# Query weights of a PEER layer through two pairs of buffers, first expert rows in other tiles

## The reference

```python
def reference(x, c, ctx, c_ctx, w_mod, ..., w_query, sub_keys, expert_u, expert_v, g_final):
    # one layer here: x and ctx are (1, 256, 2048) float32
    mod = jax.nn.silu(c) @ w_mod[l] + b_mod[l]
    sh1, sc1, ga1, sh2, sc2, ga2 = jnp.split(mod[:, None, :], N_MOD, axis=-1)
    ...                                              # context scan states, latent mixing
    y = jnp.concatenate([fourier_mix(four, g_fourier[l]), y_m], axis=-1) @ w_out[l]
    x = x + ga1 * y
    h2 = modulate(rmsnorm(x, g_norm_ffn[l]), sh2, sc2)
    x = x + ga2 * peer(h2, w_query[l], sub_keys[l], expert_u[l], expert_v[l])
    return rmsnorm(x, g_final)

def peer(...):                                       # xb: 128 tokens
    q = (xb @ w_query).reshape(PEER_BLOCK, PEER_HEADS, 2, PEER_QDIM // 2)
    s = jnp.einsum('thpd,hpnd->thpn', q, sub_keys)
    sv, si = lax.top_k(s, PEER_TOPK)
    ...                                              # 16 x 16 candidates per head
    top_s, pos = lax.top_k(cand, PEER_TOPK)
    idx = jnp.take_along_axis(cidx, pos, axis=-1)    # 16 experts per head and token
    gate = jax.nn.softmax(top_s.astype(jnp.float32), axis=-1)
    act = jax.nn.gelu(jnp.einsum('thkd,td->thk', expert_u[idx], xb).astype(jnp.float32))
    return jnp.einsum('thk,thkd->td', (gate * act).astype(xb.dtype), expert_v[idx])
```

## Time and profile before

| | before |
|---|---|
| median of 3 runs | 2023.39 us (2022.85 to 2025.05) |
| the profiled execution, its own time | 2022.52 us |
| its span | 2020.7 us |
| PE busy | 1647.9 us (82%) |
| DVE busy | 1112.4 us (55%) |
| ACT busy | 381.8 us (19%) |
| POOL busy | 695.9 us (34%) |
| moved by DMA | 723.61 MB, mean 358 GB/s |

### The profile page before, as it was taken

One profiled execution on the slowest core, in us unless ns is written; L12 is line 12 of the kernel. 1 busy time (PEld: TensorE's weight loads), 2 busy tenths in 40 slices (PEclk: granted clock), 3 DMA queues, 4 the chain that ended last, 5 costly groups with the idle time before them and its releaser, 6 DMA issues.

```text
span 2020.7 us, 13865 instructions
## 1 busy us (share of the span) xinstructions
PE 1647.9 (82%) x4619; PEld 774.8 (38%) x4619; DVE 1112.4 (55%) x1862; ACT 381.8 (19%) x1124; POOL 695.9 (34%) x572
## 2 busy tenths in 40 slices
PE   3899999998999587799997777777777777777776
PEld 0446444556446476343332222222222222222332
DVE  1158863666545858334354664655647646556444
ACT  2011003114102000222222212212213122122112
POOL 1000100000100423666663535535445455354541
PEclk7899999999999798899999999999999999999999
DMA  9979764543983977999999999999999999999996
GB/s 381 407 287 342 275 224 167 196 179 124 380 307 125 371 306 321 373 422 423 423 422 422 423 421 422 422 422 422 422 422 422 422 423 422 423 422 422 423 422 267
DMA packets 136777, 723.61 MB, mean 358 GB/s; under 512 B 10218, under 2 KB 10554, under 8 KB 69635
## 3 DMA queue, kind: packets, MB, share of 16 engines
q0 software_dynamic: 92784, 614.83, 74.2%
q1 hardware_dynamic: 43760, 107.82, 14.2%
q10 hardware_dynamic: 162, 0.08, 0.0%
HBM read 720.56 MB, written 2.13 MB: 358 GB/s over the span
## 4 chain that ended last, share of the span: by engine, by line
DMA 43%; PE 31%; DVE 12%; POOL 9%; issue 3%; SPq 1%; ACT 1%; DVEq 0%; POOLq 0%
DMA ring<-in_expert_u,acc 17%; PE ps L867 11%; DMA ring<-in_expert_v,acc 10%; DMA qh<-in_expert_u,acc 7%; POOL ring L413 6%; PE ps L992 4%; PE ps L1132 3%; DVE ring L1528 3%; DMA ring<-in_w_query 3%; DMA ring<-in_w_mod 2%; DMA H<-in_expert_v,acc 2%; PE ps L774 1%; PE ps L863 1%; PE ps L861 1%; POOL VX L413 1%
## 5 line engine op out<-in xcount | busy, mean ns | idle before, releaser
L1132 PE MATMUL ps<-ring,wg 128*128 128x512 f32 x1184 | 545.1, 606 | 163.8 <-DMA ring<-in_expert_v,acc 163.8
L1528 DVE SCALAR_TENSOR_TENSOR ring<-ring,A 128x2048 f32<-128x2048 f32 x177 | 404.1, 2293 | 381.7 <-DMA ring<-in_expert_u,acc 381.4
L1132 PEld LDWEIGHTS ps<-ring,wg 128*128 128x128 f32 x1184 | 216.9, 192 | 490.6 <-issue 307.3
L413 POOL DMA_INDIRECT ring<-in_expert_u,acc x177 | 243.7, 1377 | 393.2 <-DVE ring L1528 323.4
L1132 PE MATMUL ps<-H,wg 128*128 128x512 f32 x576 | 262.5, 600 | 67.0 <-DMA H<-in_expert_v,acc 67.0
L867 PE MATMUL ps<-ring,H 128*128 128x512 f32 x512 | 225.0, 598 | 2.2 <-ACT VX L517 2.2
L692 ACT ACTIVATE wg<-K,VX 128x128 f32<-128x128 f32 x256 | 102.8, 402 | 654.0 <-PE ps L1132 652.3
L413 POOL DMA_INDIRECT ring<-in_expert_v,acc x148 | 175.4, 1185 | 106.1 <-PE ps L1132 62.2
L1132 PEld LDWEIGHTS ps<-H,wg 128*128 128x128 f32 x576 | 104.6, 190 | 223.4 <-issue 141.8
L1155 DVE SCALAR_TENSOR_TENSOR acc<-ring,vec,acc 128x512 f32<-128x512 f32 x240 | 180.4, 752 | 11.7 <-DMA ring<-in_w_mod 3.3
L360 POOL DMA_DIRECT2D ring<-in_w_mod x32 | 28.7, 896 | 443.1 <-DVE acc L1155 342.0
(11 more groups left out here) (227 smaller groups left out, 1272.7 us busy)
## 6 DMA issues: line engine op xcount, KB each, us to landing
ring<-in_w_mod POOLq DMA_DIRECT2D x32, 2048.0 KB, 9.3
ring<-in_w_mod SPq DMA_DIRECT2D x16, 2048.0 KB, 21.7
ring<-in_w_in SPq DMA_DIRECT2D x15, 2048.0 KB, 12.4
ring<-in_w_out SPq DMA_DIRECT2D x8, 2048.0 KB, 14.1
ring<-in_w_query SPq DMA_DIRECT2D x8, 2048.0 KB, 20.2
ring<-in_expert_u,acc POOLq DMA_INDIRECT x177, 24.5
ring<-in_expert_v,acc POOLq DMA_INDIRECT x148, 25.1
B<-in_ctx SPq DMA_DIRECT2D x2, 1024.0 KB, 20.3
```

The source lines that it names most:

```text
L413: nc.gpsimd.indirect_dma_start(rows_, None, table, bass.IndirectOffsetOnAxis(ap=eidx[:, rank:rank + 1], axis=0)).then_inc(loaded, 16)
L1132: ins = mm(ps[:, 4 * b + n, :], diag[:, r % 4, :], v_rows[r % V_SLOTS][:, n * CH:(n + 1) * CH], start=k == 0, stop=k == BLOCK_RANKS - 1, s ...
L1528: v.scalar_tensor_tensor(out=rows_u, in0=rows_u, scalar=1.0, in1=A[:, r // BLOCK_RANKS, :], op0=ALU.mult, op1=ALU.mult, accum_out=dots[:, ...
```

## The change

`w_query`'s chunks alternate between two pairs of buffers: chunks 0 and 2 go to `W[2]` and `W[3]` with semaphores of their own (`q_ld`), chunks 1 and 3 to `W[0]` and `W[1]`. Chunk 0 is issued when VectorE is done with the last two halves of the modulation (`m_free` 31 and 32), chunk 1 when TensorE is done with the halves of `w_out`'s last chunk (`w_free` 39 and 40), chunk 2 at `w_free` 41 and 42, which TensorE gives when it is done with the halves of chunk 0, and chunk 3 at 43 and 44, the halves of chunk 1. Before, chunk n waited for the halves of the chunk just ahead of it, `w_free` 39 and 40 for chunk 0 to 45 and 46 for chunk 3.

Since `W[2]` and `W[3]` are rows 4 to 7 of `ring`, the first 36 U ranks use four other slots: `VX`, `gy`, the first 2048 columns of `KT`, and `gwork`, a new tile that also holds the gate tiles `gsb`, `t1`, `t2` and `negm` (in use only in the first half). From rank 36 on, U has seven slots: `ring` 4 to 7, `qh`, `VX`, `gwork`. `ga2` and the final norm's weights go into `KT` and `gy` only after that, in POOL's queue behind the gathers of U rank 43 and V rank 15 (`load_last_rows`).

```diff
--- before.py
+++ after.py
@@ -50,10 +50,11 @@
 SPREAD_ORDER = (0, 1, 2, 3)
 RANKS = TB * PH * TOPK
 BLOCK_RANKS = PH * TOPK
-EARLY = 5
+EARLY_SLOTS = (4, 7, 8, 6)
+LATE_SLOTS = (0, 1, 2, 3, 5, 4, 6)
 LEAD = 36
 LAG = 4
-U_SLOTS, V_SLOTS = 6, 7
+U_SLOTS, V_SLOTS = 9, 7
 CLOSING = 24
 SOFT_FIRST = 4
 SOFT_AT = {40: 4} | {g * TOPK + 3: g + 1 for g in range(4, TB * PH - 1)}
@@ -104,7 +105,7 @@
 
 def u_slot(r):
 
-    return r % EARLY if r < LEAD else (r - LEAD) % U_SLOTS
+    return EARLY_SLOTS[r % len(EARLY_SLOTS)] if r < LEAD else LATE_SLOTS[(r - LEAD) % len(LATE_SLOTS)]
 
 
 def lag_behind(u):
@@ -167,15 +168,14 @@
         vec = sb("vec", [P, V_ALL])
         shT = sb("shT", [P, 2, KB])
         gT = sb("gT", [P, 2, KB])
-        gsb = sb("gsb", [NG, 2 * T])
-        t1 = sb("t1", [40, 2 * T])
-        t2 = sb("t2", [40, 2 * T])
-        negm = sb("negm", [40, T])
+        gwork = sb("gwork", [P, D])
         bg = sb("bg", [NG, 1])
         uT = sb("uT", [P, 6, 40])
         st = sb("st", [P, 64])
         small = sb("small", [P, 16])
 
+        gsb, t1, t2 = gwork[0:NG, 0:2 * T], gwork[0:40, 2 * T:4 * T], gwork[0:40, 4 * T:6 * T]
+        negm = gwork[0:40, 6 * T:7 * T]
         ident = K[:, C_ID:C_ID + P]
         ones32 = K[:, C_ONE:C_ONE + 32]
         eps = K[:, C_EPS:C_EPS + 1]
@@ -225,7 +225,7 @@
         sums = VXf[:, D + 1280:D + 1296]
         eidx = flat(acc)[:, 0:256].bitcast(U32)
         u_rows = [*(ring[:, 4 + i, :] for i in range(4)), VXf[:, 0:D],
-                  qh[:].rearrange("p a b t -> p (a b t)")]
+                  qh[:].rearrange("p a b t -> p (a b t)"), gwork[:], gy[:], KTf[:, 0:D]]
         v_rows = [*(ring[:, i, :] for i in range(4)), Hf[:, 0:D], Hf[:, D:2 * D], modrow[:]]
         wgf = flat(wg)
         diag = wgf[:, 0:4 * P].rearrange("p (s n) -> p s n", s=4)
@@ -245,6 +245,7 @@
         S = {n: sem(n) for n in names}
         w_ld = [sem(f"w_ld{i}") for i in range(2)]
         m_ld = [sem(f"m_ld{i}") for i in range(2)]
+        q_ld = [sem(f"q_ld{i}") for i in range(2)]
         a_ld = [sem(f"a_ld{i}") for i in range(4)]
         u_ld = [sem(f"u_ld{i}") for i in range(U_SLOTS)]
         v_ld = [sem(f"v_ld{i}") for i in range(V_SLOTS)]
@@ -324,10 +325,19 @@
                 for i, kh in enumerate(HALVES):
                     sp.wait_ge(S["w_free"], 32 + 2 * n + i - 1)
                     load(kh, w_out[0], kh, slice(n * CH, (n + 1) * CH))
-            for n in range(4):
+            def load_query(n, kh):
+                base, loaded = (2, q_ld) if n % 2 == 0 else (0, w_ld)
+                sp.dma_start(W[base + kh], w_query[0][kh * KH * P:(kh + 1) * KH * P,
+                                                      n * CH:(n + 1) * CH].rearrange(
+                    "(k p) n -> p k n", p=P)).then_inc(loaded[kh], 16)
+
+            for kh in range(2):
+                sp.wait_ge(S["m_free"], 2 * (MODB - 1) + kh + 1)
+                load_query(0, kh)
+            for n in range(1, 4):
                 for i, kh in enumerate(HALVES):
-                    sp.wait_ge(S["w_free"], 40 + 2 * n + i - 1)
-                    load(kh, w_query[0], kh, slice(n * CH, (n + 1) * CH))
+                    sp.wait_ge(S["w_free"], 36 + 2 * n + i + 1)
+                    load_query(n, kh)
             for b in range(TB):
                 for n in range(4):
                     sp.wait_ge(S["final_ready"], 4 * b + n + 1)
@@ -374,10 +384,13 @@
             pool.dma_start(gy[:, FW:D], g_mlstm.to_broadcast([P, FW])).then_inc(S["ld_gy"], 16)
             load_from(MODB_SCAN + 1, MODB_LATE)
 
-            def spread(r, dst, loaded):
-
+            def store_row(r):
                 pool.dma_start(mod_dram[r:r + 1, :], modrow[32 * r:32 * r + 1, :]
                                ).then_inc(S["st_mod"], 16)
+
+            def spread(r, dst, loaded):
+
+                store_row(r)
                 pool.wait_ge(S["st_mod"], 16 * (SPREAD_ORDER.index(r) + 1))
                 pool.dma_start(dst, mod_dram[r:r + 1, :].to_broadcast([P, D])
                                ).then_inc(S[loaded], 16)
@@ -403,11 +416,15 @@
 
             pool.wait_ge(S["g2_ready"], 1)
             pool.wait_ge(S["modb_free"], MODB)
-            spread(3, ga2, "ld_ga2")
+            store_row(3)
             pool.wait_ge(S["keys_psum"], 16)
-            pool.dma_start(gy[:], g_final.rearrange("(a d) -> a d", a=1).to_broadcast([P, D])
-                           ).then_inc(S["ld_gfin"], 16)
-
+
+            def load_last_rows():
+                pool.wait_ge(S["u_free"], LEAD)
+                pool.wait_ge(S["st_mod"], 16 * 4)
+                pool.dma_start(ga2, mod_dram[3:4, :].to_broadcast([P, D])).then_inc(S["ld_ga2"], 16)
+                pool.dma_start(gy[:], g_final.rearrange("(a d) -> a d", a=1).to_broadcast([P, D])
+                               ).then_inc(S["ld_gfin"], 16)
 
             def gather(table, rows_, rank, loaded):
                 nc.gpsimd.indirect_dma_start(
@@ -436,6 +453,8 @@
                 gather_u(LEAD + i)
                 gather_v(2 * i)
                 gather_v(2 * i + 1)
+                if i == len(LATE_SLOTS):
+                    load_last_rows()
             r = 2 * (LEAD - LAG)
             for u in range(r + LAG, RANKS):
                 gather_u(u)
@@ -1046,12 +1065,11 @@
                     kh = HALVES[part]
                     kk = kh * KH + k
                     if k == 0:
-                        n = 0
-                        pe.wait_ge(w_ld[kh], 16 * (12 + n + kh))
+                        pe.wait_ge(q_ld[kh], 16)
                         if part == 0 and b == 1:
                             pe.wait_ge(S["qtok_ready"], h + 1)
                     ins = mm(ps[:, h, 0:T], h2T[:, kk, b * P:(b + 1) * P],
-                             W[kh][:, k, h * T:(h + 1) * T], start=step == 0, stop=step == KB - 1)
+                             W[2 + kh][:, k, h * T:(h + 1) * T], start=step == 0, stop=step == KB - 1)
                     if step == KB - 1:
                         ins.then_inc(S["qtok_psum"], 1)
                 return ins
@@ -1100,13 +1118,17 @@
                 if n == 3:
                     pe.wait_ge(S["q_free"], 2)
                 for part, kh in enumerate(HALVES):
-                    pe.wait_ge(w_ld[kh], 16 * (12 + n + kh))
+                    if n == 2:
+                        pe.wait_ge(q_ld[kh], 32)
+                    else:
+                        pe.wait_ge(w_ld[kh], 16 * (12 + n // 2 + kh))
+                    wq = W[(2 if n == 2 else 0) + kh]
                     for j in range(4):
                         for k in range(KH):
                             kk = kh * KH + k
 
                             ins = mm(ps[:, 2 * (n % 2) + j // 2, (j % 2) * T:(j % 2 + 1) * T],
-                                     W[kh][:, k, j * P:(j + 1) * P], h2T[:, kk, :],
+                                     wq[:, k, j * P:(j + 1) * P], h2T[:, kk, :],
                                      start=part == 0 and k == 0 and j % 2 == 0,
                                      stop=part == 1 and k == KH - 1, skip_group_check=True)
                     ins.then_inc(S["w_free"], 1)
```

## The result

| | before | after |
|---|---|---|
| median of 4 runs each | 2023.22 us (2022.85 to 2025.05) | 1996.28 us (1993.86 to 1997.31) |
| ratio of after to before, 95% interval | | 0.9864 (0.9852 to 0.9876) |
| the profiled execution, its own time | 2022.52 us | 1993.86 us |
| its span | 2020.7 us | 1992.1 us |
| PE busy | 1647.9 us | 1639.7 us |

The change takes 1.4% off, 27 us between the medians. The forecast was 1991.0 us, with a range from 1981 to 2003. The spans of the two profiled executions differ by 28.6 us.

The account below looks back on a forecast made before the run. The prediction took the DMA's stream of gathers at 422 to 423 GB/s as the bound, so its start counts: 36.5 us earlier less 5.0 for broadcasts is 31.5, 2022.5 to 1991.0 us; range 1981 to 2003 us.

Parts of the forecast that it names:

- Chunk 0 early: Start of the query projection: the 1.97 us wait goes and matmuls run faster; gain 2.0 to 3.7 us, taken as 3.0.
- Chunk 1 early, no wait for scores: Query projection: chunk 1 lands before TensorE needs it; TensorE's 18.98 us and VectorE's 15.34 us waits go.
- Dots 0 to 15: VectorE's first dots: four ranks at its own pace of 2.26 us, twelve at the shared 3.23; 47.8 us, until 714.7.
- Dots 16 to 31: VectorE's dots after pick 2: between 36.1 us (VectorE alone) and 47.8 (shared pace); taken as 44, until 770.1.
- Chunks 2 and 3: Last query chunks: chunk 3 done at 762.4, its scores at 765.6, before dots end at 770.1, so dots set the start.
- Rival 3: Chunk 3's weights come late, scores at 785, rank 36 lands at 791: 2001 us; chance 0.13.
- The late stream: Gathers from rank 36 on: POOL no longer waits for dot 35; rank 36 lands at 780.8, 36.5 us before 817.3.
- It goes on: Late stream at the eighth V: its data can run 2 to 3 us before the queue empties; nothing charged.
- rival 2: The stream begins early but runs dry at the eighth V, DMA empty for 5 to 12 us: 1999 us; chance 0.12.
- The slower rival: TensorE stays at the lower clock for V rows after idling; 20 such rows would give 2057 us; chance 0.04.
- The broadcasts: Two 1.05 MB row loads, formerly in idle time, now stand in the full stream and cost 5.0 us.
- The seventh late slot: The extra U slot in the late stream is worth nothing where the DMA is already full.

Follow-up runs that it names:

- e5: The change, but chunk 0's halves issued late, as before, with the other chunks at their new times: 1998.45 us, ratio to before 0.9876.
- e3: The changed kernel with each half of w_query loaded at its old time, slots and buffers as changed: 2030.68 us, ratio to before 1.0035.
- e7: The changed kernel with ring rows as slots from U rank 20 on, six slots in place of four: 1985.97 us, ratio to before 0.9808.
- e2: The changed kernel without the two broadcast loads and the waits for them: 1988.74 us, ratio to before 0.9828.
- e6: The changed kernel with six late U slots instead of seven, gwork left out: 1994.54 us, ratio to before 0.9845.
- e1: The changed kernel run again unaltered: 1993.29 us, ratio to before 0.9847.

## Why the prediction was right, and where its steps were off

The measured 1996.28 lies in the range, 5.3 us above the forecast, and the likeliest case is the one that happened. By its steps, in the profile after, counted from the first query matmul (628.71, before 632.40) so that the 3.7 us ahead of it are out:

- **Chunk 0 early: 3.0 us forecast, 3.9 measured.** Pick 0 starts 10.9 us after the first query matmul (639.59), before 14.8 (647.20). It is a little above the upper bound of 3.7. How much of it reaches the end is open: e5 puts it at 3.9 by medians and at 1 to 2 by its profile.
- **Chunk 1 early, no wait for scores: as forecast.** The waits of 18.98 and 15.34 us are gone. e3 shows that all of the gain hangs on the early loads of the four chunks together (37.4 us), and e5 that some 4 us of that or less are chunk 0's.
- **Dots 0 to 15: 47.8 us forecast, 51.6 measured.** This is the step that failed most. I took the shared pace for all ranks behind the first four. But gather 4 can be issued only behind dot 0, at 664.85, and it shares the DMA with the gathers ahead of it and with chunk 2's weights (issued at 654.0 and 661.0, landed at 671.5 and 694.5). It lands in 10.5 us while dots 1 to 3 need 6.6: a wait of 4.11 at rank 4, where with five slots ranks 4 and 5 had waited 0.55 and 1.07. Rank 20's gather, issued behind dot 16 in the same way but with an almost idle DMA, took 7.3 us. The landings of these two, and the DMA at the time:

```profile
DMA to landing us min/median/max: 10.5/10.5/10.5
665.00:675.00 10.00, 10.00 (x48) 8.81 (x47) 6.22 (x6) 0.00 (x0) 7.35 (x4) 1.00 1.03 404
...
DMA to landing us min/median/max: 7.3/7.3/7.3
726.00:730.00 4.00, 4.00 (x20) 3.54 (x19) 4.00 (x5) 0.10 (x1) 2.17 (x1) 1.00 0.09 34
```

- **Dots 16 to 31: 44 us forecast, 45.8 measured,** within the bounds. The lower bound of 36.1 was nearly the right price for enough slots: e7 has 35.4, a dot every 2.21 us.
- **Chunks 2 and 3: done by 765.6 forecast, 756 measured.** Rival 3, weights late next, did not come: no wait ahead of either chunk. The weights were in fact much earlier than in the sum: chunk 2's halves landed at 671.5 and 694.5 (687 and 711 forecast) and chunk 3's at 717.8 and 728.1 (734 for the first). It did no harm, since the dots set the start.
- **The late stream: 36.5 us forecast, 30.1 measured.** Rank 36 was issued 2.4 us behind dot 31's end (771.06), not 1.3, for POOL was itself busy: four gathers ahead took 2.11 to 2.99 us each beside dots. Its rows, the yardstick, landed 10.0 us later, at 783.5: 33.8 us before 817.3, or 30.1 without the 3.7 ahead of the first query matmul. (Rank 38's dot, the first in the late stream that waited for its rows, gives 31.1: 798.42 against 833.26 before.) The 6.4 that are missing are the dots (3.8 and 1.8), POOL (1.1) and rank 36's landing (0.6: 10.0 us for 9.4 in the sum), less the 0.9 of chunk 0.
- **It goes on: right.** POOL stood 8.61 us at the eighth V and the DMA stayed at 421 GB/s; rival 2 had its wait but not its price. The slower rival did not come either. TensorE had idled 36.59 us and its clock was 0.51 in the window up to 797, the lower level (1.2 GHz), but 1.00 in the one from 797, and the DMA stayed full.
- **The broadcasts: 5.0 us forecast, 4.6 measured** (e2).
- **The seventh late slot: nothing, as forecast** (e6).

Together: 30.1 less 5.0 is 25.1, which is what the two profiles show when counted from the first query matmul (24.9). So part of the nearness to the forecast is luck: in the profiled pair, the 3.7 us ahead of the changed code make up for more than half of the 6.4 that the steps fell short. The medians give the change 26.9 us in the first measurement and 29.6 in the second (e1), against 31.5 forecast.

Two rules were weighed. The first is the fit of 2.0 us plus bytes over 436 GB/s for a transfer (the Trainium skill, "DMA: Bandwidth & Descriptors", section "Anatomy of one DMA — SWDGE (gpsimd) path", an estimate of 4.4 us for a gather). The prediction set it against landings of 8.2 and 10.2 us, but both were of gathers that shared the DMA. The fairest case after is the very first gather, issued at 651.79 into an idle DMA: it landed in 5.8 us, the shortest in that profile and still 1.4 above the estimate. Where it mattered the fit does not hold: gather 4 took 10.5 us and gather 35 took 8.5.

The second is the lock-out of GpSimd (the Trainium skill, "SBUF — State Buffer", section "SBUF: two separate sides"). It goes with what the issues show, 0.94 us alone and 1.9 to 3.0 beside dots. But for a VectorE operation with two SBUF inputs, as the dots are, that section names a conflict only with a GpSimd operation that reads SBUF, and whether the issue of a gather does so no run here shows; nor does any isolate the port as the cause.

## What to carry to other kernels

Where a stream at the limit of the DMA ends the kernel, ask only when it becomes full, and count bytes and idle time up to there: beside gathers of 8 KB rows at 324 GB/s the loads of 2 KB rows got some 90 here, so they belong ahead of the gathers. Count the slots of a ring against the order of the engine that frees them: one slot less cost 27.5 us here, most of it because the last gather fell behind a long step. Buffers that a change takes away may be free again a few steps later; giving them back brought another 9 us (e7).

## What the runs showed of the hardware that was not expected

- How long an indirect gather of 1.05 MB takes from issue to landing hangs on what else is under way: 5.8 us into an idle DMA with no dots running (rank 0 after), 7.3 us into an almost idle one beside dots (rank 20 after, 34 GB/s), 10.5 us beside other gathers, weights and dots (rank 4 after, 404 GB/s), 28.3 us at the median of the whole run. 2.5 us of it are transfer at 422 GB/s.
- Its issue on POOL takes 0.94 us while VectorE waits or picks, and 1.91 to 3.0 us while dots run back to back (e7: 1.91 or 1.90 for eleven in a row).
- The profiled executions of kernels that are alike up to there differed by 4 us at the first query matmul (628.7 to 632.9).
